# HGRN decays in a fused two-block kernel: a tree of gate products, one level of all heads at a time, in place of exponentials of summed logarithms

## The reference, cut to what matters

```python
f  = lb + (1 - lb) * sigmoid(f_raw)        # the decay gate, per token and feature (as log_f)
kk = (1 - lb) * sigmoid(-f_raw)
qq = silu(q_raw)
# S_t = diag(f_t) S_{t-1} + kk_t v_t^T ;  o_t = q_t S_t, which is, for every pair of tokens s <= t:
A[t, s] = sum_e q[t, e] * exp(b[t, e] - b[s, e]) * k[s, e]      # b = cumsum(log f)
o[t]    = sum_s A[t, s] * v[s]
```

## Time and profile before

| | |
|---|---|
| Time of the runs | 1281.52 us median of 3 (1280.45, 1281.52, 3279.57) |
| The profiled execution | 1281.95 us, its span from first to last instruction 1280.1 us |
| Granted clock of TensorE | 0.999 of full speed (2.4 GHz) over the span |
| Busy | PE 99%, DVE 70%, ACT 55%, POOL 13% of the span |
| Moved by DMA | 221.77 MB, 173 GB/s on average |

### The profile page before, as it was taken

How to read it: one execution, slowest core, us unless ns; L and a number is a source line. 1 busy time by engine, 2 the same in 40 slices (tenths; PEclk the granted TensorE clock), 3 DMA queues, 4 the chain that set the end, 5 groups by cost and what they waited for, 6 DMA issues and landing times.

```text
span 1280.1 us, 23610 instructions
## 1 busy us (share of the span) xinstructions
PE 1268.5 (99%) x9664; PEld 1193.6 (93%) x9664; DVE 899.7 (70%) x1588; ACT 708.9 (55%) x1150; POOL 164.6 (13%) x208
## 2 busy tenths in 40 slices
PE   9999999999999999999999999999999999999997
PEld 7889778999999988899999999999998889999997
DVE  7988798877665478767666556666557876766652
ACT  7665574655554585556554445554467546655542
POOL 4102400383001100013000110000120001200001
PEclk9999999999999999999999999999999999999999
DMA  9536644566565451436665565656545134655660
GB/s 329 200 110 194 209 153 127 180 202 195 197 204 193 148 182 64 132 120 195 198 195 187 188 198 189 198 193 204 196 149 181 58 126 130 194 189 194 198 196 36
DMA packets 61499, 221.77 MB, mean 173 GB/s; under 512 B 7120, under 2 KB 7376, under 8 KB 61136
## 3 DMA queue, kind: packets, MB, share of 16 engines
q1 hardware_dynamic: 60768, 219.00, 52.1%
q0 software_dynamic: 336, 1.11, 0.4%
q10 hardware_dynamic: 288, 0.16, 0.1%
HBM read 219.20 MB, written 1.05 MB: 172 GB/s over the span
## 4 chain that ended last, share of the span: by engine, by line
PE 90%; DVE 7%; issue 1%; ACT 1%; POOL 1%; DMA 0%; POOLq 0%; ACTq 0%; DVEq 0%
PE pb L485 13%; PE pb L487 13%; PE pb L486 13%; PE pb L500 8%; PE pb L501 7%; PE pb L502 7%; PE pb L469 7%; PE pb L471 6%; PE pb L470 6%; PE pb L558 2%; DVE s_wl L1308 2%; PE pb L608 2%; DVE s_acc L1448 2%; PE pb L731 1%; PE pb L587 1%
## 5 line engine op out<-in xcount | busy, mean ns | idle before, releaser
L1308 DVE TENSOR_TENSOR s_wl<-s_wraw,s_wh 128x1024 fp32r<-128x1024 f32 (+1 forms) x411 | 506.7, 1254 | 106.3 <-ACT s_wh L911 106.1
L911 ACT ACTIVATE s_wh<-s_wraw 128x1024 fp32r<-128x1024 f32 (+1 forms) x411 | 420.9, 1049 | 163.7 <-PE pb L487 86.1
L485 PE MATMUL pb<-s_xh,s_wh 128*128 128x256 f32 x1408 | 390.9, 278 | 0.0
L487 PE MATMUL pb<-s_xh,s_wl 128*128 128x256 f32 x1408 | 390.0, 277 | 0.0
L486 PE MATMUL pb<-s_xl,s_wh 128*128 128x256 f32 x1408 | 389.8, 277 | 0.0
L486 PEld LDWEIGHTS pb<-s_xl,s_wh 128*128 128x128 f32 x1408 | 264.8, 188 | 0.0
L485 PEld LDWEIGHTS pb<-s_xh,s_wh 128*128 128x128 f32 x1408 | 264.8, 188 | 0.0
L487 PEld LDWEIGHTS pb<-s_xh,s_wl 128*128 128x128 f32 x1408 | 264.6, 188 | 0.0
L469 PE MATMUL pb<-s_wh,s_xh 128*128 128x512 f32 x448 | 182.5, 407 | 1.1 <-DVE s_wl L1308 1.1
L500 PE MATMUL pb<-s_hh,s_wh 128*128 128x256 f32 x660 | 182.2, 276 | 0.0
L501 PE MATMUL pb<-s_hl,s_wh 128*128 128x256 f32 x660 | 182.2, 276 | 0.0
(11 more groups left out here) (311 smaller groups left out, 1584.0 us busy)
## 6 DMA issues: line engine op xcount, KB each, us to landing
s_wraw<-in_w SPq DMA_DIRECT2D x407, 512.0 KB, 4.2
s_nab<-in_rpb SPq DMA_DIRECT2D x2, 1024.0 KB, 9.6
s_x<-in_x SPq DMA_DIRECT2D x4, 256.0 KB, 5.5
out_dram<-s_at_s SPq DMA_DIRECT2D x4, 256.0 KB, 2.1
s_cst<-in_cst SPq DMA_DIRECT2D x1, 684.0 KB, 9.6
s_mlev<-in_lev POOLq DMA_DIRECT2D x1, 576.0 KB, 4.9
s_wraw<-in_w SPq DMA_DIRECT2D x2, 256.0 KB, 4.6
s_ln<-in_lng POOLq DMA_DIRECT2D x2, 128.0 KB, 7.2
```

What stands on the lines that cost most here:

```text
L485: pe.matmul(o, wh[:, s, w], x_block(xh, n, k), start=k == v == 0, stop=False, skip_group_check=True)
L487: r = pe.matmul(o, wl[:, s, w], x_block(xh, n, k), start=False, stop=k == 7, skip_group_check=True)
L911: return act.activation(o, src, ACT.Copy, scale=scale)
L1308: dve.tensor_tensor(wl[:, s, part], wraw[:, r, part], wh[:, s, part].bitcast(F32), ALU.subtract).then_inc(low_done, 1)
```

## The change

The gate is no longer turned into a logarithm. The raw sigmoid `fg` is transposed (eight transposes a layer, `f0` and `f1`, at tile 12), DVE makes the gate from PSUM into `fd` with features on the partitions and all four heads side by side, and six pairwise products build a tree in `span`: the product of the gates over blocks of 2, 4, ... 64 tokens. `qd` and `kd` (the two halves of `qkt`) are queries and keys of all heads, with features on the partitions. The queries take the gate of their own token once. Then for m = 1, 2, ... 64 PE multiplies keys by queries at that level for all heads (`level(i)`), and `advance(i)` on DVE multiplies in place the queries of each second block by the product over the first block, and the keys of each first block by the product over the second. `level(7)` is the step between the halves. `lb1`, the constant `mlev` (its transfer of 576 KB becomes one of 4 KB for `freq`), the logarithms, the split, `exponents`, `exs` and the exponentials are gone. Matmuls of keys by queries keep their shapes and their number: 8 a level of m = 1 to 16, 16 for m = 32, 8 for m = 64, 4 for the step between the halves, a layer. Buffers behind `mlev` move down by 4608 bytes a partition.

```diff
+            tiles(n, 12)
+            pe.wait_ge(fsig_done, 2 * l + 2)
+            for j in range(2):
+                turn_block(n, f"f{j}", lambda t, p: fg[:, t, hd(2 * j + p)])
             for h in range(4):
-                tiles(n, 22 + h)
+                tiles(n, 20 + h // 2 * 2)
...
+                turn_block(n, f"qk{h}", lambda t, p: (qq, kk)[p][:, t, hd(h)])
+            tiles(n, 26)
...
+            def level(i):
+                m = 1 << i
+                pe.wait_ge(level_ready, 8 * l + i + 1)
+                o = claim(n, f"m{i}")
+                for h in range(4):
+                    if m == P:
+                        r = pe.matmul(o[:, hd(h)], kd[:, h, 0:P], qd[:, h, P:TOKENS], start=True, stop=True)
+                        continue
+                    for t in range(2):
+                        keys, queries = kd[:, h, P * t:P * (t + 1)], qd[:, h, P * t:P * (t + 1)]
+                        at = 2 * h + t
...
+                        else:
+                            r = pe.matmul(o[:, 64 * at:64 * (at + 1)], keys, level_view(queries, m)[:, :, 1, :], start=True,
+                                          stop=True)
+                r.then_inc(*fill(n, f"m{i}"))
...
+            for h in range(4):
+                name = f"f{h // 2}"
+                dve.wait_ge(*full(n, name))
+                i = dve.tensor_scalar(fd[:, h, :], psum(n, name)[:, TOKENS * (h % 2):TOKENS * (h % 2 + 1)],
+                                      lbc[:, l, 0, h:h + 1], lbc[:, l, 1, h:h + 1], ALU.mult, ALU.add)
...
+            for i in range(6):
+                if i:
+                    dve.wait_ge(span_done, 6 * l + i)
+                pairs = fall(i).rearrange("p (b s) -> p b s", s=2)
+                dve.tensor_tensor(fall(i + 1), pairs[:, :, 0], pairs[:, :, 1], ALU.mult).then_inc(span_done, 1)
...
+            dve.tensor_tensor(flat(qd), flat(qd), flat(fd[:, :, :]), ALU.mult).then_inc(level_ready, 1)
...
+            def advance(i):
+                m = 1 << i
+                dve.wait_ge(*full(n, f"m{i}"))
+                dve.wait_ge(level_ready, 8 * l + i + 1)
+                dve.wait_ge(span_done, 6 * (l + 1))
+                base = qkt[:, 0, 0, m:2 * m]
+                both = bass.AP(base.tensor, base.offset, [list(base.ap[0]), [2 * m, 2 * TOKENS // m], [4 * TOKENS - m, 2], [1, m]])
+                factor = fall(i).rearrange("p (b s) -> p b s", s=2).unsqueeze(3).to_broadcast([P, 2 * TOKENS // m, 2, m])
+                dve.tensor_tensor(both, both, factor, ALU.mult).then_inc(level_ready, 1)
...
+                    b = lambda ap: ap.rearrange("p a (b i) -> p a b i", i=m)
+                    dve.copy_predicated(
+                        a.rearrange("p a (b s i) -> p a b s i", s=2, i=m)[:, :, :, 1, :],
+                        b(msk[:, 4 - i, :].unsqueeze(1).to_broadcast([P, 8, 64])),
+                        b(o[:, :].rearrange("p (a q) -> p a q", a=8))).then_inc(*empty(n, name))
```

More of the change, by code:

```diff
@@ L706, in mixers2 @@
             hd = lambda h: slice(P * h, P * (h + 1))
-            def exponents(h, t):
-                if h == 0 and t == 0:
-                    pe.wait_ge(lf_done, 2 * l + 2)
-                    if l == 0:
-                        pe.wait_ge(ld_lev, 16)
-                for j in range(2):
-                    name = f"e{h}{t}" + "ab"[j]
-                    m = mlev[:, P * t + NCOL * j:P * t + NCOL * (j + 1)]
-                    o = claim(n, name)
-                    pe.matmul(o[:, :], lfh[:, t, hd(h)], m, start=True, stop=False)
-                    pe.matmul(o[:, :], lfl[:, t, hd(h)], m, start=False, stop=True).then_inc(*fill(n, name))
@@ L800, in mixers2 @@
                                  fill(n, name) if h and t else None)
-            tiles(n, 28)
-            exponents(0, 0)
-            exponents(0, 1)
+            tiles(n, 27)
+            level(0)
             tiles(n, 29)
@@ L807, in mixers2 @@
             score_fox(0)
-            exponents(1, 0)
-            exponents(1, 1)
+            level(1)
             tiles(n, 31)
-            levels(0, 0)
-            levels(0, 1)
+            level(2)
             tiles(n, 33)
             turn_weights(n, "F", 0)
-            cross(0)
-            tiles(n, 34)
-            exponents(2, 0)
-            exponents(2, 1)
+            level(3)
             tiles(n, 35)
@@ L839, in mixers2 @@
             turn_block(n, "yF", lambda t, p: fo[:, t, P * p:P * (p + 1)])
-            tiles(n, 41)
-            cross(2)
-            tiles(n, 44)
-            levels(3, 0)
-            levels(3, 1)
+            level(7)
             tiles(n, 45)
@@ L848, in mixers2 @@
             turn_block(n, "lk", lambda t, p: dlqk[:, t, 256 + P * p:256 + P * (p + 1)])
-            tiles(n, 46)
-            cross(3)
             tiles(n, 49)
@@ L868, in mixers2 @@
             pe.wait_ge(*gone(n, ("in", 6, 1)))
-            pe.wait_ge(*gone(n, "l31"))
-            for h in range(4):
-                pe.wait_ge(*gone(n, f"x{h}"))
+            pe.wait_ge(*gone(n, "m6"))
+            pe.wait_ge(*gone(n, "m7"))
             for t in range(2):
@@ L1144, in mixers2 @@
             act.wait_ge(*gone(n - 1, ("out", 3)))
-            for j in range(2):
-                act.wait_ge(*full(n, f"lb{j}"))
-                copy(lbb[:, j, :], psum(n, f"lb{j}")[:, :]).then_inc(*empty(n, f"lb{j}"))
+            act.wait_ge(*full(n, "lb"))
+            copy(lbb, psum(n, "lb")[:, :]).then_inc(*empty(n, "lb"))
             split(n, 6)
@@ L1763, in mixers2 @@
                                              dia[:, t, h:h + 1]).then_inc(dia_done, 1)
+            split(n, 17)
+            for h in range(4):
+                dve.wait_ge(*gone(n, f"qk{h}"))
+            dve.tensor_tensor(flat(qd), flat(qd), flat(fd[:, :, :]), ALU.mult).then_inc(level_ready, 1)
             split(n, 18)
@@ L1889, in mixers2 @@
             turn_dilated(1)
-            split(n, 26)
-            blocks(3, 0)
-            blocks(3, 1)
+            y_low(n, "yF", y2, 0)
             split(n, 27)
```

293 lines of the change are left out of this document (89 added, 204 removed), and 8 rows, old and new, of the table MISC.

## The result

The changed kernel takes 1262.36 us, the median of 4 runs (1261.65 to 1262.61), for 1281.56 us before measured beside it: a ratio of 0.9852 (95% interval 0.9833 to 0.9871), or 19 us. One of the four runs of the kernel before took 3279.57 us; nothing on record says why, and the median doesn't hang on it. The profiled execution after took 1262.19 us, its span is 1260.4 us.

A forecast was written before the change was run, and what follows sets the result against it. PE was taken as the bound, busy 1268.5 of 1280.1 us. Removed exponents -15.9, transposes +0.8 and turns -0.9 summed to -16.0 us, giving 1265.5 us from the runs' median 1281.52; range 1262.5 to 1272.5.

The forecast's parts named there:

- Turns: First projection matmul after each fp32 piece costs 0.09 us extra; five fewer pieces a layer, -0.9 us over two layers.
- (1): The gate's transposes at tile 12 wait for ACT's sigmoid; expected hidden, as four logarithms no longer run.
- (2): DVE work from the gate's transposes to the first level: an estimated 5 us added for some 9 us removed.
- (5): First fq transpose at tile 26 waits for ACT's four fqk copies, as before; ACT has one key copy less ahead.
- (3): Chain of levels: each next level waits for advance, 1.25 us; the two shortest gaps leave 1.6 us or more.
- (4): Budget from level(0)'s end to level(7)'s start: DVE 27 us against PE 38.6; with upper-end prices DVE 40.6.
- (6): DVE's copy of the second half's turned attention weights ends about 0.8 us before PE weighs; the thinnest margin.
- The rule that spoke against it: SBUF needs two hits per 16-byte line for full speed; by it advance(0) and advance(1) would cost over 1.25 us.
- A: Rival: one to three of hand-offs (6), (3), (5) miss by 0.5 to 1.5 us a layer; costs 1 to 7 us; 0.13.
- B: Rival: DVE's chain between level(0) and level(7) becomes the bound; 11 us a layer late, 1287 us; chance 0.03.
- C: Rival: hh and hl, moved by 4608 bytes, slow 2112 matmuls by 5 ns each; +10.6 us, 1276 us; chance 0.06.
- D: Rival: time per key-by-query matmul changes with the new order, -3 to +1 us; 0.77 together with the forecast.

The follow-up runs named there:

- e2_sums_back: The changed kernel plus 64 fp32r matmuls of 512 columns whose results are overwritten: 1276.05 us, 0.9948 of the kernel before.
- e1_regroup: The kernel before, with the key-by-query matmuls of a head's two halves grouped by shape: 1280.29 us, 0.9981 of the kernel before.
- e7_merge: The changed kernel with three fp32 pieces a layer joined to others: 1262.37 us, 0.9842 of the kernel before.
- e4_delay1: The changed kernel with one more unused DVE product of 1024 elements ahead of each advance: 1265.56 us, 0.9860 of the kernel before.
- e9_early: The changed kernel with DVE's copy of the second half's turned attention weights moved ahead of unit 24: 1261.22 us, 0.9836 of the kernel before.
- e5_delay3: The changed kernel with three more unused DVE products of 1024 elements ahead of each advance: 1295.72 us in a single execution.
- e3_pad: The changed kernel with 4608 unused bytes a partition in mlev's place, so later buffers lie as before: 1263.21 us, 0.9847 of the kernel before.

## Why the prediction was right, and which step was not

**The bound.** Right: PE alone sets the end, and 19.7 us less for PE are 19.7 us less of the span. e2_sums_back shows it in the other direction. The fall of PE from 159.6 to 151.6 us that the prediction looked for was read off a stretch that runs 12 us too far; over the phase itself it is 146.78 to 137.52. DVE fell by 14 us in each mix phase, not by 20, and ACT by 12 to 13, as said; neither shows in the time.

**What PE loses.** 64 matmuls at 0.235 us and the gap were 15.9 us, measured 16.0.

**What PE gains.** The transposes came to +0.7 for +0.8. The step that failed is the one behind it: "The matmuls of keys by queries (L727, L731, L737) are as many as before and of the same shapes; only their order changes", and then "I cost that at 0", with -3 to +1 as bounds. It measured -5.3 us, outside its own bounds. (The bounds were loose themselves: 160 records at 0.11 instead of 0.125 us give -2.4, and nothing in the working gives +1.) I had priced records by their mean in a row of mixed shapes and looked for the bound at the pace of the widest alone; the six records of L727 at 0.45 us stood in the earlier trace rows with a mean of 0.075 us, and what they would take without their neighbours (0.020 and 0.067) was not asked. e1_regroup shows 0.4 us a head from the grouping alone, in the kernel before. This one term is the largest error of the forecast. The others are 1.2 us for the other small pieces, 1.0 for the phases outside and some -0.5 for small misses in the exponents, the transposes and the turns: 1265.5 - 5.3 + 1.2 + 1.0 - 0.5 = 1261.9, measured 1262.36. The mechanism was right, and that the time came out only 3.1 us off, at the very edge of the range, is luck in part: 2.2 us that nobody had reckoned with covered some of the 5.3.

**Turns.** -0.9 us forecast, -1.2 in the projection's steps; e7_merge got nothing for six of them. The price was read on one side only. The eight transposes of the earlier trace rows take 0.79 us and not 8 x 0.11 because their last record is short; a joined piece loses that, so most of the term was none.

**New waits.** (1), (2) and (5) hid as said. (3) and (4): the stretch came out at 27.6 against 35.9 us; `advance` was right for six of seven sizes, 0.9 us too cheap at m = 1, and the masked copy 0.47 too cheap at m = 1 and 2 and 0.15 too dear beyond; the errors partly cancelled in the sum and were covered by the 8 us of room, which e4_delay1 shows to be just used up by 8.5 us. (6) was the thinnest margin, as said; the 0.8 us reckoned weren't there, and its wait costs 0.23 us a layer by e9_early.

**The rule that spoke against it.** It held at m = 1, chiefly in writing, the side that the prediction left open, and a little in reading (0.24 us), where the prediction took L1786 to speak against it. It didn't hold for advance(1), which the prediction had put under it too: 1.23 us. To reckon all sizes by L1308's row was wrong at m = 1, and it was right that this would not decide.

**Rivals.** A came only as the one wait of (6), 0.5 us in all and under its 1 to 7, hidden by a larger gain. B did not come; e5_delay3 shows that it would have, at 1295.7 us, with 25.6 us more on DVE a layer. C is refuted by e3_pad and the unchanged pace of L478. D was the right place, in the direction of a gain, and larger than its bounds.

## What to carry to other kernels

Price small matmuls by their shape and their neighbours, not by the mean of a mixed row: group those with the same number of weight columns, and where blocks of a masked product let 32 weight columns do, cut them so that they go to different groups of 32 output partitions (that the groups are what pays is inferred, that the cut pays is measured). Here it was worth 8.6 us by the mix phases on top of a change that gave 19 (1252.6 us, 0.9765 of the kernel before). Read a piece's price from its first start to the start of what follows, on both sides: what one side seems to save, the other may pay. When a serial chain between two engines replaces bulk work, add up both engines' work over the stretch of the chain; the surplus is the room. It held to about a microsecond in two runs; when the sums are nearly even, look at each link by itself.

## What the runs showed of the hardware

- fp32 matmuls with 32 weight columns, spread over four groups of output partitions: 64 records in 0.66 us with 16 moving columns, 32 in 1.01 us with 128. With 128 weight columns a record takes 0.10 to 0.11 us, with 64 0.067.
- The last record of a piece of fp32 transposes: a step of 0.03 us ahead of an fp32r matmul, 0.11 ahead of fp32 with as many weight columns, 0.20 ahead of fewer (32). The fp32r matmul behind an fp32 piece steps by 0.31 to 0.32 us for 0.23.
- DVE in place on two alternating places of one element each: 2.08 to 2.16 us for 1024 elements instead of 1.23; 1.99 with only the writes alternating, 1.47 with only the reads.
- A masked copy of 512 elements with runs of one or two: 1.29 to 1.32 us; with runs of four or more 0.69 to 0.72; a plain copy 0.69 at runs of one, two and four.
